# Three direct tiles per feed-forward layer instead of four, their low parts written by VectorE, and another split of the last tiles' tokens

## The reference

```
def swiglu_ffn(h, w_in, w_out):
    g, u = jnp.split(h @ w_in, [D_FF], axis=-1)      # D_FF = 2816 = 22 tiles of 128
    return (jax.nn.silu(g) * u) @ w_out
y = y + swiglu_ffn(rmsnorm(y, norm_ffn[i]), w_ffn_in[i], w_ffn_out[i])
...
y_prompt, y_sample = rmsnorm(yp, norm_final), rmsnorm(ys, norm_final)
```

## Time and profile before

| | |
|---|---|
| median of 3 runs | 1266.92 us (1265.86 to 1270.38) |
| the profiled execution | 1267.35 us |
| its span, first to last instruction | 1265.5 us |
| PE busy | 1243.5 us, 98% |
| PEld busy | 1198.7 us, 95% |
| DVE busy | 866.6 us, 68% |
| ACT busy | 621.4 us, 49% |
| POOL busy | 405.4 us, 32% |

### The profile page before, as it was taken

One profiled execution on the slowest core, in us unless ns is written; L12 is line 12 of the kernel. 1 busy time (PEld: TensorE's weight loads), 2 busy tenths in 40 slices (PEclk: granted clock), 3 DMA queues, 4 the chain that ended last, 5 costly groups with the idle time before them and its releaser, 6 DMA issues. The chain is left out here.

```text
span 1265.5 us, 23666 instructions
## 1 busy us (share of the span) xinstructions
PE 1243.5 (98%) x9354; PEld 1198.7 (95%) x9354; DVE 866.6 (68%) x1535; ACT 621.4 (49%) x1158; POOL 405.4 (32%) x255
## 2 busy tenths in 40 slices
PE   8999999999999999999999999999999999999996
PEld 8888899999999999998889998899989999999996
DVE  5776757982288877768547887678962288876655
ACT  5565544562277756642023454225452277766631
POOL 1000034423322222246665544465313322222141
PEclk9999999999999999999999999999999999999998
DMA  9511121272267777733232332223262277677722
GB/s 327 171 35 51 52 64 70 68 171 96 67 160 172 154 167 169 163 117 112 74 112 76 117 137 90 88 72 116 88 142 92 72 159 171 161 166 165 167 84 76
DMA packets 54318, 152.28 MB, mean 120 GB/s; under 512 B 7504, under 2 KB 11536, under 8 KB 52768
## 3 DMA queue, kind: packets, MB, share of 16 engines
q1 hardware_dynamic: 33968, 107.30, 26.3%
q0 software_dynamic: 16704, 30.42, 14.8%
q10 hardware_dynamic: 3536, 13.05, 2.9%
HBM read 143.27 MB, written 9.44 MB: 121 GB/s over the span
## 5 line engine op out<-in xcount | busy, mean ns | idle before, releaser
L684 POOL TENSOR_TENSOR wlo<-wst,whi 128x1024 fp32r<-128x1024 f32 x85 | 212.6, 2501 | 331.5 <-ACT whi L2282 328.8
L728 PE MATMUL ps<-xhi,whi 128*128 128x288 f32 x688 | 209.1, 304 | 1.1 <-DVE wlo L1426 0.7
L729 PE MATMUL ps<-xlo,whi 128*128 128x288 f32 x688 | 202.9, 295 | 0.0
L730 PE MATMUL ps<-xhi,wlo 128*128 128x288 f32 x688 | 202.2, 294 | 0.0
L693 POOL DMA_DIRECT2D wlo<-w_blocks_in x80 | 69.3, 866 | 304.9 <-ACT wlo L2357 293.5
L728 PEld LDWEIGHTS ps<-xhi,whi 128*128 128x128 f32 x688 | 129.0, 187 | 9.6 <-issue 8.3
L728 PE MATMUL ps<-hid,whi 128*128 128x288 f32 x448 | 132.6, 296 | 1.3 <-POOL wlo L684 1.3
L729 PE MATMUL ps<-hid,whi 128*128 128x288 f32 x448 | 132.9, 297 | 0.0
L730 PE MATMUL ps<-hid,wlo 128*128 128x288 f32 x448 | 132.5, 296 | 0.0
L728 PE MATMUL ps<-bhi,whi 128*128 128x288 f32 x432 | 128.9, 298 | 3.1 <-DMA wlo<-w_blocks_in 3.1
L729 PEld LDWEIGHTS ps<-xlo,whi 128*128 128x128 f32 x688 | 129.3, 188 | 0.2
(11 more groups left out here) (351 smaller groups left out, 3511.0 us busy)
## 6 DMA issues: line engine op xcount, KB each, us to landing
wst<-w_blocks_in SPq DMA_DIRECT2D x188, 512.0 KB, 3.6
wlo<-w_blocks_in POOLq DMA_DIRECT2D x80, 256.0 KB, 4.1
more_lo<-w_blocks_in POOLq DMA_DIRECT2D x36, 256.0 KB, 6.2
S<-s_in ACTq DMA_DIRECT2D x4, 1024.0 KB, 5.0
s_sample_out<-S ACTq DMA_DIRECT2D x4, 1024.0 KB, 4.7
y_out<-x SPq DMA_DIRECT2D x16, 144.0 KB, 1.9
bias<-bias_in SPq DMA_DIRECT2D x1, 2048.0 KB, 11.3
x<-x_in SPq DMA_DIRECT2D x4, 288.0 KB, 6.8
```

The source lines that it names most:

```text
L684: nc.gpsimd.tensor_tensor(lo, wst[:, slot, :], raw(hi), ALU.subtract).then_inc(w_split, 1)
L728: mm(out, stat[0], mov[0], start=start, stop=False, skip_group_check=skip)
L729: mm(out, stat[0], mov[1], start=False, stop=False, skip_group_check=skip)
L730: return mm(out, stat[1], mov[0], start=False, stop=stop, skip_group_check=skip)
```

## The change

- `N_DIRECT` is 3 instead of 4: tile 3 of each layer becomes a unit, the first of its series.
- The lows of the direct blocks from the third on (four a layer) are written by VectorE (`block_low` in its `ffn`) instead of GpSimd, each at a written place in VectorE's list, which is reordered around them.
- In that first unit A11's low is written by VectorE (`first_a11_low`), and A12 and A22 come by adding DMA.
- ScalarE's order in the units: the next unit's A11 comes first (before the copy of product 1), S3 after it; A22's negative is written after the hidden tile's high; in the first out unit the highs of T2 and T3 come first. `copy` of products 1 and 6 waits for the top halves instead of the corner of the unit before.
- The lows of the last six down blocks of layer 1 are written by VectorE instead of GpSimd.
- The last two output tiles are cut into 384 and 192 tokens instead of 288 and 288. Three of the eight scaled tiles of the first part are done by ScalarE (gain) and GpSimd (multiplication), and stored by ACT.

```
-N_DIRECT = 4
+N_DIRECT = 3
 def by_transfer(q, u):
+    if u == UNITS[0]:
+        return q != "A11"
     return u not in FIRST and not (q == "A22" and u in LAST)
...
+TOKENS = (slice(0, 3 * P), slice(3 * P, N))
+COLS = ([(c * P, P) for c in range(3)], [(0, P), (P, NS_TOK)])
+BY_POOL = (0, 1, 2)
...  # SP
+            for i, (a, m) in enumerate([(0, m) for m in range(3, KC)] + [(1, m) for m in range(KC)]):
+                sp.wait_ge(y_done, i + 1)
+                sp.dma_start(io["y"][:, m, TOKENS[a]], x[:, m, TOKENS[a]]).then_inc(s_y, 16)
...  # GpSimd, ffn
-                for n in range(B_F1[l], IN_AT[l][N_DIRECT]):
-                    split(n)
+                split(B_F1[l])
+                split(B_F1[l] + 1)
                 for ph, us in zip(DOWN_OF, SERIES):
-                    quarter_low("A11", l, us[0])
+                    if ph:
+                        quarter_low("A11", l, us[0])
...
                     for n in DOWN_AT[l][ph]:
-                        split(n)
+                        if not by_vector(n):
+                            split(n)
...  # tensor engine, last_down
-                            if a == 1 and i == 0 and c == 3:
-                                last_sums(0)
-                            if a == 1 and i == 1 and c == 4:
-                                spread(0, 6)
                         ins.then_inc(last_half, 1)
+                        if a == 1 and i == 0:
+                            last_sums(0)
...
+                spread(0, 6)
                 last_sums(1)
+                pe.wait_ge(last_read, 2)
+                spread(0, 2)
                 spread(1, 7)
...  # VectorE, ffn
+                def block_low(n):
+                    dve.wait_ge(act_split, NOT_OWN.index(n) + 1)
+                    dve.wait_ge(*split_of(n - 1))
+                    hi, lo = ring(n)
+                    tt(lo, wst[:, n % STAGE, :], raw(hi), ALU.subtract).then_inc(w_split, 1)
...
+                late = range(B_F1[l] + 2, IN_AT[l][N_DIRECT])
                 gate(0)
                 normed_x(0, 4)
+                block_low(late[0])
+                normed_x(4, KC)
                 up(0)
-                normed_x(4, KC)
-                hidden_low(0)
-                gate(1)
+                block_low(late[1])
                 dve.wait_ge(x_normed, KC * (l + 1))
                 token_sum("T1", b12, x11)
                 token_sum("T3", x22, b12)
-                up(1)
+                hidden_low(0)
+                gate(1)
+                block_low(late[2])
...
+                up(1)
+                block_low(late[3])
+                operand_low("B11")
+                operand_low("B21")
                 hidden_low(1)
                 gate(2)
-                operand_low("B11")
-                operand_low("B21")
-                up(2)
+                sum_s1(first)
+                first_a11_low(first)
+                sum_s2(first)
                 operand_low("T1")
-                sum_s1(first)
-                hidden_low(2)
-                gate(3)
-                sum_s2(first)
+                sum_low("S1", first)
                 operand_low("T2")
-                sum_low("S1", first)
-                operand_low("B22")
                 sum_s4(first)
                 sum_low("S2", first)
-                up(3)
+                up(2)
+                operand_low("B22")
...  # ScalarE, the loop over units
-                        copy(1, u)
-                        if u not in FIRST:
-                            quarter_high("S3", u)
-                        if f is not None and not first_half(f):
+                        if fresh_out:
                             sum_high("T2", f)
                             sum_high("T3", f)
-                        if nxt is not None:
+                        if u not in FIRST and nxt is not None:
                             quarter_high("A11", nxt)
+                        copy(1, u)
                         if u in FIRST:
+                            quarter_high("A11", nxt)
                             quarter_high("S4", u)
...
+                        else:
+                            if heavy and not fresh_out:
+                                sum_high("T2", f)
+                                sum_high("T3", f)
+                            quarter_high("S3", u)
+                            copy(5, u)
```

More of the change, by code:

```diff
@@ L1667, in sum_s3, with first_a11_low @@
                     weight_sum("S3", u, stage(u, "11"), stage(u, "21"), ALU.subtract)
+                def block_low(n):
[3 more added lines that the diff above has]
+                    tt(lo, wst[:, n % STAGE, :], raw(hi), ALU.subtract).then_inc(w_split, 1)
+                def first_a11_low(u):
+                    hi, lo, _ = quarter("A11", l)
+                    dve.wait_ge(q_hi["A11"], ordinal(l, u))
+                    tt(lo, stage(u, "11"), raw(hi), ALU.subtract).then_inc(q_lo["A11"], 1)
                 def last_a22_low(u):
@@ L1758, in down @@
                     tt(cols(x, m), pair(2 * (m % 2)), cols(x, m), ALU.add).then_inc(added(l, ph, m)[0], 1)
+                    if l and ph:
+                        n = DOWN_AT[1][2][m + 2]
+                        dve.wait_ge(act_split, NOT_OWN.index(n) + 1)
+                        tt(wlo[:, n % RING, :], wst[:, n % STAGE, :], raw(whi[:, n % RING, :]), ALU.subtract
+                           ).then_inc(late_lows, 1)
                     if ph:
@@ L2135, in _ @@
             diagonal(0)
+            last_tile(1, 1)
             dve.wait_ge(rb_done, 1)
-            last_tile(1, 1)
-            for m in range(3):
+            scaled(0, 3)
+            scaled(0, 4)
+            diagonal(1)
+            for m in range(5, KC):
                 scaled(0, m)
-            diagonal(1)
-            for m in range(3, KC):
-                scaled(0, m)
-            dve.wait_ge(rb_done, 2)
+            dve.wait_ge(rb_done, 3)
             for m in range(KC):
@@ L2355, in quarter_high, with a22_negative @@
                     fn(hi, flat, ACT.Copy).then_inc(q_hi[q], 1)
-                    if q[0] == "A" and by_transfer(q, u):
+                    if q in ("A11", "A12") and by_transfer(q, u):
                         fn(lo, flat, ACT.Copy, scale=-1.0).then_inc(q_neg[q], 1)
+                def a22_negative(u):
+                    if by_transfer("A22", u):
+                        n = blocks_of(l, u)[1]
+                        fn(quarter("A22", l)[1], wst[:, n % STAGE, 512:1024], ACT.Copy, scale=-1.0
+                           ).then_inc(q_neg["A22"], 1)
                 def copy(i, u):
@@ L2371, in ffn @@
                 silu(0)
+                operand_high("B11")
                 late_split(ahead[1])
+                operand_high("B21")
+                operand_high("B22")
                 hidden_high(0)
[L2374 removed]
+                operand_high("T1")
                 late_split(ahead[2])
                 silu(1)
[L2377 to L2381 removed]
                 operand_high("T3")
                 operand_high("T2")
+                late_split(ahead[3])
                 operand_high("T4")
[L2385 removed]
+                hidden_high(1)
+                quarter_high("A11", first)
                 silu(2)
[L2387 to L2391 removed]
+                quarter_high("S1", first)
+                quarter_high("A12", first)
                 quarter_high("S2", first)
@@ L2396, in ffn @@
                         f = prev[1] if in_halves(prev) else None
-                        copy(1, u)
-                        if u not in FIRST:
-                            quarter_high("S3", u)
-                        if f is not None and not first_half(f):
+                        fresh_out = u == ("out", 1, 0)
+                        light = f is not None and first_half(f)
+                        heavy = f is not None and not light
+                        if fresh_out:
                             sum_high("T2", f)
```

109 lines of the change are left out of this document (56 added, 53 removed).

## The result

The kernel before ran at 1267.92 us (median of 20 runs), the changed one at 1269.83 (median of 20). The ratio is 1.002, 95% interval 1.0012 to 1.0028: slower by 1.5 to 3.5 us, which is within half a per cent. The forecast of 1267.3 us was 2.5 us low; the measured time lies in its range.

What follows compares the result with a forecast made beforehand. The prediction took the tensor engine as the bound, busy 1243.5 of 1265.5 us. Its terms, -3.2 + 7.7 + 3.0 - 4.3 + 2.2 - 1.5 - 3.5, gave +0.4 on 1267.35, less 0.43 to the median: 1267.3 us, range 1261 to 1273.

Steps and rivals of the forecast that it cites:

- 1. One tile fewer: Direct tile turned seven-product unit: 84 matmuls instead of 96, 24 fewer over two layers, -3.2 us.
- 2. The third block's wait: Third direct block of each layer waits for its low, behind gate(0) and four normed_x on VectorE: +7.7 us.
- it fits by 1.9 us: VectorE's list up to the first unit's S3 low takes 33.1 us of 35.0, so no further stall charged.
- 3. The clock: After the third block's stall, one stretch at half clock in each layer: +3.0 us, bounds 0 and 4.
- 4. The first pairs: A11's waits and their clock loss go at the first pairs, 1.2 us of waits left: -4.3 us.
- 5. Order in the pairs: S3's later high delays the first out units, +2.2 us; A11's earlier issue ends the third out units' waits, -1.5.
- 6. The end: Last low's wait goes and the output tail shortens with 384/192 token tiles and shared stores: -3.5 us.
- (a): At the third block the stall comes but the clock holds: 1264.3 us, chance 0.20.
- (b): The third block does not wait, as its low is not placed last: 1256.6 us, chance 0.09.
- (c): Third-block stall only: clock holds, no leftovers at the first pairs or first out units: 1260.9 us, chance 0.09.
- (d): VectorE falls behind at the first pair; products 3, 7 and 4 wait, clock falls again: 1274.3 us, chance 0.14.
- Steps 3, 4 and 5: Half clock after third-block waits; third pair's A11 waits at most 1 us; first out unit two about 1 us, third none.

Runs made afterwards that it cites:

- run 4: Kernel before with only the third direct block's low moved to VectorE, behind gate(0) and four normed_x: 1277.96 us, ratio 1.0073.
- run 1: Changed kernel with the third direct block's low written by GpSimd again: 1262.56 us, ratio 0.9959 against the kernel before.
- run 3: Changed kernel with 24 unused matmuls run ahead of the third block's wait in each layer: 1265.14 us, ratio 0.9983 against the kernel before.
- run 10: Kernel before with only ScalarE's new order in the units: 1264.48 us, ratio 0.9978.
- run 5: Changed kernel with S3's high ahead of A11's again in each layer's first out unit: 1269.22 us, ratio 1.0013 against the kernel before.
- run 11: Changed kernel with GpSimd writing the third and fourth direct blocks' lows, and S3's high ahead of A11's in the first out unit: 1262.29 us.
- run 12: Changed kernel with GpSimd writing the third and fourth direct blocks' lows, first out unit's order as changed: 1263.74 us, ratio 0.9971 against the kernel before.
- run 9: Kernel before with the whole new end, token parts and VectorE's lows of the last down blocks: 1265.12 us, ratio 0.9981.
- run 6: Changed kernel with the first unit's A22 low by GpSimd's subtraction instead of the adding DMA: 1271.1 us, ratio 1.0024 against the kernel before.
- run 8: Kernel before with only the lows of the last down blocks moved to VectorE: 1266.42 us, ratio 0.9992.
- run 7: Kernel before with only the end's token parts of 384 and 192, with GpSimd's, ScalarE's and ACT's share: 1266.21 us, ratio 0.999.

## Why the prediction was right, and where its terms were off

The class and the range held. The parts all had the right sign; against the profiled executions their errors add up to +3.5 us, less the 0.8 that the balance leaves over. The class is 6.3 us wide to each side, so it would have borne such errors either way.

**1. One tile fewer** (-3.2): 24 matmuls fewer in the program's count. Right as far as the count goes; no run isolates its time.

**2. The third block's wait** (+7.7): 7.3, by the links that the prediction listed. Run 4 shows that this low alone makes the kernel before slower, run 1 that it is the cause in the changed kernel. What was wrong is "it fits by 1.9 us": with the wait taken away (run 1), VectorE is 1.3 to 1.9 us late at the next block. I had summed the list up to its last item only, and not at each block on the way. It did no harm to the forecast, since the wait at the third block was there.

**3. The clock** (+3.0): 5.2 in the profiled execution, the term with the largest error there. That both layers pay was right; the length of a stretch was taken from the one of before, 3.4 us, and after the longer waits it was 6.83 in both layers. It is not so in every execution: by the mean clocks most had less (2.7 to 5.2, above), and run 3 puts the price near 4 by medians. So the 3.0 is at the low end, not wrong in kind. Taken with the lost 1.5 of before, the profiled clock is a net +3.7.

**4. The first pairs** (-4.3): -3.1. A11's waits and the clock there went, as forecast, and run 10 shows that ScalarE's order does it. The 1.2 us left for leftovers became 2.4. The issue ahead of need was right (5.1 us, forecast 5), but these transfers land after 5.8 us in the median (6.0 at the first unit, in both layers), and the rows that I used give 4.8.

**5. Order in the pairs** (+2.2 and -1.5): +1.8 and -1.5. The two waits came where forecast, at T2's last low and h2lo, 0.9 us a layer in place of 1.1. The traces of runs 5, 11 and 12 show that they come from the order there, and that the third out unit doesn't need it; the times of these runs don't resolve it. Run 10 shows the gain there without anything else of the change.

**6. The end** (-3.5): -2.6 by the trace, -2.2 by run 9's medians. The low's wait went. I had SP's last eight stores 0.5 us apart; their starts, 1261.98 to 1266.25, span 4.3 us instead of 3.5, and the end comes 2.3 us behind the last of them instead of 2.05: 1.0 us, about the whole miss. The narrow matmuls (below) cost 0.9 us where I had taken 0.6. The diagonals did not meet GpSimd: they end at 1259.99, its first multiplication starts at 1260.30.

Of the rivals, (a), the held clock, is excluded by the windows, (b) by the waits. (c) needs (a). (d) did not come: products 3 and 7 do not wait, and product 4 waits under 1 us, for its add's landing and not for VectorE's list. Where VectorE does run late, once the third block's wait is gone, is the fourth block.

Of the signs, the wait of layer 0 (4.58 us) lies above the 3.5 to 4 and that of layer 1 (3.32) below. With the slow clock behind them the first product starts at 241.93, 6.4 us earlier than before and not 7 to 9. From the last down matmul to the span's end are 11.5 us instead of the 10 to 11. Steps 3, 4 and 5 came as listed, step 5 with 0.71 and 0.54 us.

## What to carry to other kernels

A subtraction that moves to a faster engine is placed by what stands ahead of it there: 1.22 us instead of 2.40 was written 5 us later. Check such a list at every block that waits for it, and again with the first wait taken away, for a long wait hides the next ones. The waits of 3 us or more on the tensor engine cost their length and, in this kernel, 1.3 to 2.7 us of slow clock on top. A transfer that is issued a fixed time ahead of need, 5.1 us here, costs what its landing takes beyond that, which was 0.6 to 2.4 us for product 4 of layer 0 (landings of 5.7 to 7.5 us in runs 3 and 11).

## What the runs showed of the hardware

- The half-clock stretch has no fixed length. After the same wait of 4.58 us in layer 0 it was 6.83 us (the changed kernel, run 4) or 3.41 us (runs 5 and 6), after that of 3.32 us in layer 1 it was 6.83 (the changed kernel, run 5) or 3.41 (runs 4 and 6). Nor does a wait of a given length decide whether there is one: at the third pair of layer 1 the kernel before lost 2.31 us and had 3.41 us of half clock, run 9 lost 2.25 there and run 8 2.45, both at 1.00 throughout; run 7, with 3.29, had 6.83. Waits of 2.17 and 2.49 us (run 11) were followed by none. What decides stays open. The wait of run 9 and its windows:

```profile
930.84 0.37 PE L742 MATMUL ps<-bhi,whi 128*128 128x288 f32 x1 [2.10 <-DMA wlo<-w_blocks_in]
...
928.60:930.84 2.24, 0.14 (x3) 0.03 (x1) 2.14 (x5) 0.42 (x1) 0.35 (x1) 1.00 1.11 205
930.84:937.00 6.16, 6.16 (x46) 6.16 (x47) 2.23 (x4) 3.38 (x8) 0.86 (x1) 1.00 0.62 150
```

- At full clock a matmul of 384 columns starts every 176 ns and one of 192 every 112 ns (the changed kernel, 1252 to 1257), beside 133 for 288. In proportion to columns the second would be 89.
- The adding DMA of 256 KB that brings A22 lands 4.7/5.8/7.0 us after its issue, those of A11 and A12 4.5 us in the median; the issue holds GpSimd for 0.86 us. That of the first unit in layer 0 landed after 6.0 us in the changed kernel, 6.7 in run 1 and 7.5 in run 11, and product 4 started about 0.1 us later each time.
